# Attention scores in fewer shapes: decode queries laid out block-diagonally, prompt products alternating between halves

## The reference

```python
# differential attention: two score maps per head, each over 64 of the 128 head columns
a = probs(q[..., :64], k[..., :64]) - lam * probs(q[..., 64:], k[..., 64:])
out_da = a @ v
# multi-head latent attention: 128 columns without rotation and 64 rotated ones, the rotated key shared by all heads
k_m = concat([kv[..., :128], broadcast(k_rope)], axis=-1)
s = (q_m @ k_m.T) * 192 ** -0.5
out_mla = softmax(mask(s)) @ v_m
```

## Time and profile before

| what | value |
|---|---|
| median of three runs | 2510.61 us (2506.28 to 2514.45) |
| profiled execution, first to last instruction (its span) | 2504.7 us |
| TensorE busy | 2453.5 us, 98% of the span |
| chain of work that ended last, TensorE's share | 95% |
| VectorE, ScalarE, GpSimd busy | 1186.1, 801.0, 138.6 us |
| 16 DMA engines, share of the span on the weights' queue | 41.8% |
| mean granted TensorE clock | 0.992 |

### The profile page before, as it was taken

The page is one execution under the profiler, slowest core; times in us unless marked ns, Lnnn a source line. Parts: engine busy times, 40 slices in busy tenths (PEclk is TensorE's granted clock), DMA queues, the critical chain, the costliest instruction groups (busy, mean ns, idle before and its releaser), DMA issues.

```text
span 2504.7 us, 36768 instructions
## 1 busy us (share of the span) xinstructions
PE 2453.5 (98%) x16307; PEld 2389.8 (95%) x16307; DVE 1186.1 (47%) x892; ACT 801.0 (32%) x686; POOL 138.6 (6%) x59
## 2 busy tenths in 40 slices
PE   7999999999999999999999989999999999999998
PEld 5999999999999999989899669999999999999998
DVE  6444444444444447345484226444444444444445
ACT  3322322232323224333333224323322332233223
POOL 2000000000000001000000001000000000000001
PEclk9999999999999999999999899999999999999999
DMA  5444444444444444515153113444444444444441
GB/s 193 152 152 151 151 150 145 145 147 149 150 151 151 151 150 152 162 62 179 55 151 119 42 43 118 152 152 151 150 145 147 146 150 150 151 151 151 151 147 64
DMA packets 178896, 345.98 MB, mean 138 GB/s; under 512 B 10383, under 2 KB 17046, under 8 KB 178518
## 3 DMA queue, kind: packets, MB, share of 16 engines
q1 hardware_dynamic: 175942, 337.11, 41.8%
q0 software_dynamic: 2160, 7.60, 0.9%
q10 hardware_dynamic: 736, 0.41, 0.1%
HBM read 339.45 MB, written 5.65 MB: 138 GB/s over the span
## 4 chain that ended last, share of the span: by engine, by line
PE 95%; DVE 3%; ACT 1%; DMA 0%; issue 0%; SPq 0%; DVEq 0%; ACTq 0%
PE ps L1202 29%; PE ps L1203 29%; PE ps L1204 29%; DVE mov_lo L822 2%; DVE w_lo L805 1%; PE ps L1554 1%; PE ps L1553 1%; PE ps L1383 1%; PE ps L1381 0%; DMA work<-in_x_sample 0%; PE ps L1278 0%; PE ps L1564 0%; PE ps L1412 0%; PE ps L1579 0%; PE ps L1428 0%; PE ps L1238 0%
## 5 line engine op out<-in xcount | busy, mean ns | idle before, releaser
L1202 PE MATMUL ps<-mov_hi,w_hi 128*128 128x320 f32 x3568 | 1108.3, 311 | 9.6 <-DVE w_lo L805 8.6
L1203 PE MATMUL ps<-mov_lo,w_hi 128*128 128x320 f32 x3568 | 1104.4, 310 | 0.0
L1204 PE MATMUL ps<-mov_hi,w_lo 128*128 128x320 f32 x3568 | 1104.2, 309 | 0.0
L805 DVE TENSOR_TENSOR w_lo<-raw,w_hi 128x2048 fp32r<-128x2048 f32 x313 | 717.3, 2292 | 744.7 <-ACT w_hi L499 744.6
L499 ACT CAST w_hi<-raw 128x2048 fp32r<-128x2048 f32 x313 | 596.8, 1907 | 1429.0 <-PE ps L1204 1428.9
L1202 PEld LDWEIGHTS ps<-mov_hi,w_hi 128*128 128x128 f32 x3568 | 671.7, 188 | 12.7 <-issue 10.3
L1203 PEld LDWEIGHTS ps<-mov_lo,w_hi 128*128 128x128 f32 x3568 | 671.6, 188 | 0.5
L1204 PEld LDWEIGHTS ps<-mov_hi,w_lo 128*128 128x128 f32 x3568 | 671.5, 188 | 0.0
L1202 PE MATMUL ps<-h_hi,w_hi 128*128 128x320 f32 x1488 | 462.9, 311 | 4.7 <-DVE h_lo L894 4.7
L1203 PE MATMUL ps<-h_lo,w_hi 128*128 128x320 f32 x1488 | 462.4, 311 | 0.0
L1204 PE MATMUL ps<-h_hi,w_lo 128*128 128x320 f32 x1488 | 462.3, 311 | 0.0
(11 more groups left out here) (193 smaller groups left out, 835.9 us busy)
## 6 DMA issues: line engine op xcount, KB each, us to landing
raw<-in_ffn_w_gate SPq DMA_DIRECT2D x88, 1024.0 KB, 5.2
raw<-in_ffn_w_up SPq DMA_DIRECT2D x88, 1024.0 KB, 5.2
raw<-in_ffn_w_down SPq DMA_DIRECT2D x88, 1024.0 KB, 5.1
raw<-in_w_in SPq DMA_DIRECT2D x28, 1024.0 KB, 5.3
raw<-in_w_out SPq DMA_DIRECT2D x16, 1024.0 KB, 5.1
raw<-in_mla_w_uq SPq DMA_DIRECT2D x12, 256.0 KB, 4.2
raw<-in_w_in SPq DMA_DIRECT2D x4, 640.0 KB, 4.1
work<-in_x_prompt SPq DMA_DIRECT2D x2, 1024.0 KB, 6.4
```

The lines of the kernel that those rows point to most:

```text
L805: dve.tensor_tensor(w_lo[:, n % SPLIT_SLOTS, :], raw[:, n % RAW_SLOTS, :], w_hi[:, n % SPLIT_SLOTS, :].bitcast(F32), ALU.subtract).then_in ...
L1202: pe.matmul(out, w[0], x[0], start=first, stop=False)
L1203: pe.matmul(out, w[0], x[1], start=False, stop=False)
L1204: return pe.matmul(out, w[1], x[0], start=False, stop=last)
```

## The change

For differential attention the decode queries of a head are laid out once as a block-diagonal 128 x 128 matrix in a new region `D_QD` (half 0's 64 rows in columns 0 to 63, half 1's in columns 64 to 127, the rest zero). GpSimd zeroes the region once per half of the heads, after the cache transposes that used it are drained; ScalarE makes two copies into it; TensorE waits for them (`qd_set`) before the first head's scores. The products over the cache and over the new keys are then one of 128 rows each, where there were two of 64 rows, and they come first. The four prompt products follow, in turn half 0 and half 1. For the latent heads VectorE makes such a matrix of the rotated decode queries (`M_QRD`) with one memset and two copies, and `mla_scores` is put in another order: the four unrotated prompt products, the four unrotated decode products (which alternate between the two column halves), two products of 128 rows for the rotated decode part of both heads, and the four rotated prompt products, alternating between row halves.

```diff
--- before.py
+++ after.py
@@ -108,9 +108,10 @@
 F_GS, F_H, F_SQ, F_ACC, F_V, F_T = 6144, 7424, 8704, 9984, 11264, 11584
 D_QT, D_KT, D_VTOK, D_CKT, D_CV, D_P, D_AT, D_DG, D_CST, D_O0 = (
     0, 1280, 2560, 4096, 6144, 8192, 10880, 11584, 12160, 14208)
-D_VT, D_KTOK, D_O1 = D_CST, D_P, D_P
+D_VT, D_KTOK, D_O1, D_QD = D_CST, D_P, D_P, D_CST + 1280
 M_QN, M_QR, M_KN, M_VM, M_KR, M_P, M_AT, M_DG = 0, 2560, 3840, 7168, 10752, 11584, 12928, 14336
 M_CQ, M_CKV, M_KRAW, M_SQ, M_V, M_Y, M_T, M_CTOK = 0, 3840, 4480, 4800, 6080, 6400, 6720, 9472
+M_QRD = 14976
 M_SQ2, M_CCT, M_CCKV, M_CKR, M_RT = 7168, 8192, 11584, 12608, 13120
 PW = 1344
 
@@ -196,6 +197,8 @@
         job_ready = sem("job_ready")
         job_drained = sem("job_drained")
 
+        qd_zero = sem("qd_zero")
+        qd_set = sem("qd_set")
         scores_ready = sem("scores_ready")
         biased = sem("biased")
         max_ready = sem("max_ready")
@@ -461,6 +464,9 @@
 
                     pool.wait_ge(job_drained, 10 * hf + 3)
                     store_tokens([D_KTOK + UC * t for t in range(3)], UC, UC * hf, kp, ks, k_stored)
+
+                    pool.wait_ge(job_drained, 10 * hf + 7)
+                    pool.memset(wk(D_QD, UC), 0.0).then_inc(qd_zero, 1)
                     pool.wait_ge(job_drained, 10 * hf + 10)
                     store_tokens([D_VTOK + UC * t for t in range(3)], UC, UC * hf, vp, vs, v_stored)
 
@@ -649,6 +655,13 @@
                     for hh in range(HB):
                         n = 10 * hf + 3 + hh
                         drain_job(n, wk(D_CKT + PAST * hh, PAST), ps[:, job_bank(n), :])
+                    act.wait_ge(qd_zero, hf + 1)
+                    act.wait_ge(drained, GR_Z + 3 * hf + 1)
+                    for half in range(2):
+                        d = slice(HALF * half, HALF * half + HALF)
+                        last = act.copy(wk3(D_QD, 4, P, d)[:, :, DEC * half:DEC * half + DEC],
+                                        wk3(D_QT, 4, T, d)[:, :, SEQ:T])
+                    last.then_inc(qd_set, 1)
                 if j == 3:
                     da_exps(HB * hf)
 
@@ -1120,11 +1133,18 @@
                 dve.wait_ge(unit_used, U_UQ + j + 1)
                 dve.tensor_copy(wk3((M_QR, M_QN, M_QN + 4 * T)[j], 4, T), bank4(GR_UQ + j)).then_inc(drained, 1)
             next_lo(U_OA2)
+            dve.wait_ge(o_lo_done, 2)
+            link(dve.memset(wk(M_QRD, 4 * P), 0.0))
             dve.wait_ge(swap_ready, 2)
             dve.tensor_tensor(wk3(M_RT, 4, T), bank4(GR_ROPE), over(sin, 4), ALU.mult).then_inc(drained, 1)
             link(dve.tensor_tensor(wk3(M_QR, 4, T), wk3(M_QR, 4, T), over(cos, 4), ALU.mult))
             dve.wait_ge(drained, GR_ROPE + 1)
-            dve.tensor_tensor(wk(M_QR, 4 * T), wk(M_QR, 4 * T), wk(M_RT, 4 * T), ALU.add).then_inc(roped, 1)
+            link(dve.tensor_tensor(wk(M_QR, 4 * T), wk(M_QR, 4 * T), wk(M_RT, 4 * T), ALU.add))
+            for half in range(2):
+                d = slice(ROPE * half, ROPE * half + ROPE)
+                last = dve.tensor_copy(wk3(M_QRD, 4, P, d)[:, :, DEC * half:DEC * half + DEC],
+                                       wk3(M_QR, 4, T, d)[:, :, SEQ:T])
+            last.then_inc(roped, 1)
             dve.wait_ge(n_hi, 2)
             dve.tensor_tensor(latents(h_lo)[:, :, 0:T], wk3(M_CKV, 2, T), latents(h_hi)[:, :, 0:T].bitcast(F32),
                               ALU.subtract)
@@ -1375,13 +1395,15 @@
 
                         pe.wait_ge(biased, h)
                     hh, b = h % HB, scores_half(hf)
-                    for half in range(2):
-                        d = slice(HALF * half, HALF * half + HALF)
-                        q, k = wk(D_QT + T * hh, T, d), wk(D_KT + T * hh, T, d)
-                        pe.matmul(ps[:, b + half, 0:SEQ], q[:, P:SEQ], k[:, 0:SEQ], start=True, stop=True)
-                        pe.matmul(ps[:, b + half, SEQ:PH], q[:, 0:P], k[:, 0:P], start=True, stop=True)
-                        pe.matmul(ps[d, b + 2, :], q[:, SEQ:T], wk(D_CKT + PAST * hh, PAST, d), start=True, stop=True)
-                        ins = pe.matmul(ps[d, b + 3, 0:DEC], q[:, SEQ:T], k[:, SEQ:T], start=True, stop=True)
+                    qd = wk(D_QD + P * hh, P)
+                    pe.matmul(ps[:, b + 2, :], qd, wk(D_CKT + PAST * hh, PAST), start=True, stop=True)
+                    pe.matmul(ps[:, b + 3, 0:DEC], qd, wk(D_KT + T * hh + SEQ, DEC), start=True, stop=True)
+                    for at, rows, keys in ((0, slice(P, SEQ), SEQ), (SEQ, slice(0, P), P)):
+                        for half in range(2):
+                            d = slice(HALF * half, HALF * half + HALF)
+                            q, k = wk(D_QT + T * hh, T, d), wk(D_KT + T * hh, T, d)
+                            ins = pe.matmul(ps[:, b + half, at:at + keys], q[:, rows], k[:, 0:keys],
+                                            start=True, stop=True)
                     ins.then_inc(scores_ready, 1)
 
 
@@ -1395,6 +1417,7 @@
                     turn_cache(hh)
                 z_unit(3 * hf + 2, 2)
                 pe.wait_ge(job_drained, 10 * hf + 7)
+                pe.wait_ge(qd_set, hf + 1)
                 da_scores(HB * hf)
                 z_unit(3 * hf + 2, 3)
 
@@ -1541,17 +1564,32 @@
 
                         pe.wait_ge(exp_done, c)
                     pr = c - HEADS
+                    news, olds = slice(SEQ, T), slice(T, NTOK)
+                    blocks = ((0, slice(P, SEQ), slice(0, SEQ)), (SEQ, slice(0, P), slice(0, P)))
+
+                    def qn(half, q):
+                        return wk(M_QN + T * (2 * pr + half), T)[:, q]
+
+                    def kn(half, k):
+                        return wk(M_KN + NTOK * (2 * (pr % 2) + half), NTOK)[:, k]
+
                     for half in range(2):
-                        d = slice(64 * half, 64 * half + 64)
-                        qn = wk(M_QN + T * (2 * pr + half), T)
-                        kn = wk(M_KN + NTOK * (2 * (pr % 2) + half), NTOK)
-                        qr, kr = wk(M_QR + T * pr, T, d), wk(M_KR, NTOK, d)
-                        for out, q, k in ((ps[:, half, 0:SEQ], slice(P, SEQ), slice(0, SEQ)),
-                                          (ps[:, half, SEQ:PH], slice(0, P), slice(0, P)),
-                                          (ps[d, 2, :], slice(SEQ, T), slice(T, NTOK)),
-                                          (ps[d, 3, 0:DEC], slice(SEQ, T), slice(SEQ, T))):
-                            pe.matmul(out, qn[:, q], kn[:, k], start=True, stop=False)
-                            ins = pe.matmul(out, qr[:, q], kr[:, k], start=False, stop=True)
+                        for at, q, k in blocks:
+                            pe.matmul(ps[:, half, at:at + k.stop], qn(half, q), kn(half, k), start=(at == 0), stop=False,
+                                      skip_group_check=True)
+                    for bank, k in ((2, olds), (3, news)):
+                        for half in range(2):
+                            d = slice(64 * half, 64 * half + 64)
+                            pe.matmul(ps[d, bank, 0:k.stop - k.start], qn(half, news), kn(half, k), start=True,
+                                      stop=False, skip_group_check=True)
+                    for bank, k in ((2, olds), (3, news)):
+                        pe.matmul(ps[:, bank, 0:k.stop - k.start], wk(M_QRD + P * pr, P), wk(M_KR, NTOK)[:, k],
+                                  start=False, stop=True, skip_group_check=True)
+                    for at, q, k in blocks:
+                        for half in range(2):
+                            d = slice(64 * half, 64 * half + 64)
+                            ins = pe.matmul(ps[:, half, at:at + k.stop], wk(M_QR + T * pr, T, d)[:, q],
+                                            wk(M_KR, NTOK, d)[:, k], start=False, stop=True, skip_group_check=True)
                     ins.then_inc(scores_ready, 1)
 
                 def mla_transpose(c):
```

## The result

The changed kernel takes 2473.78 us (median of four runs, 2472.91 to 2483.58), beside 2509.59 us for the kernel before (median of four): a ratio of 0.9871 with a 95% interval of 0.9847 to 0.9895. The profiled execution has a span of 2472.3 us, 32.4 less than before's 2504.7. The remaining 3.4 us lie in where the two profiled executions fall among their runs: the median is 4.9 us above before's span and 1.5 above the span after.

A forecast was written before the change was run, and what follows sets the result against it. TensorE's own list was taken as the bound: 9.0 us saved in differential attention plus 11.5 in latent, other engines at 0, make 20.5 off the 2510.6 median, so 2490 us, range 2480.5 to 2499.5.

The forecast's parts named there:

- bounds of the one unknown cost: Alternating array halves in both score routines: gain 13 us if each step costs a change of shape, 25 us if halves overlap.
- I take the middle, covered loads and no overlap: Score routines: products on alternating halves run one after another with loads hidden; four prompt products take 1.30 us.
- rival 2: Score routines: products on different halves of the array overlap, 25 us gain in all, 2485.5 us; chance 0.33.
- Where the softmax chain would take time back: Differential attention, `da_values`: TensorE waits 0.35 us for one head and 0.3 for the next, 0.65 us per half.
- 6 instead of 2: Sign in `da_values`: waits of some size for ScalarE's copies rise to 6 from 2, some 1.3 us more.
- The costs put at nothing: Added memsets and copies on GpSimd, ScalarE and VectorE: price 0; without cover up to 2 us and 1.5 us.
- The same total, plus or minus 4 us: Half-clock time over the run: total cost taken as unchanged, within 4 us, though where the stretches fall was unknown.
- Rival 5: Attention part: the half-clock mechanism alone makes the kernel slower, needing 56 more us at 1.2 GHz; chance 0.03.
- the case that it described: Score routines: alternating halves neither costs nor overlaps, 2490 us, own range 2485 to 2495; chance 0.42.

## Why the prediction was wrong

The step that failed is the choice in **bounds of the one unknown cost**: "I take the middle, covered loads and no overlap". The nearest rows were products of one shape on the whole array, each on the same 128 rows and columns as the one ahead of it. They say nothing on products that use different halves. The term that this put in the sum was 1.30 us for the four prompt products of a head or pair and 1.95 us for the four 64-wide ones; they take 0.76 and 1.03 us (0.85 and 1.12 with the drain behind them). The other end of that bound, rival 2, had been worked out and given 0.33; the groups by shape (5.6 instead of 11.1 us at the same count and mean) and the starts show that it is what happens.

*Rival 2's size.* It was priced as 25 us less, with the second record of one product beside the first of the next. The records pair fully: both halves start 7 ns apart and go on together. The 64-wide group of a pair takes 1.12 us (1367.33 to 1368.45), 1.03 without the drain, where rival 2 had 1.4; the rotated prompt group takes 0.85, 0.76 without it, where rival 2 had 0.9. So a pair gives 4.5 us instead of 2.88 (forecast) or 3.8 (rival 2): latent part 18.0 instead of 11.5.

*The heads.* From the product before it to the product behind it a head is shorter by 2.04 us instead of the forecast 1.39, and behind `da_transpose` by 1.77 instead of 1.19. Eight heads give 15.2, the waits take back 4.4, which leaves 10.8 beside the 10.7 from the starts, and 9.0 forecast. Where the softmax chain would take time back was right, at `da_values` of the first two heads of each half, and so was how it starts (VectorE's bias step with no idle time left). The waits are longer (1.49 and 0.75 us instead of 0.35 and 0.3), because TensorE's list moved up further than thought and VectorE's chain could not follow. "6 instead of 2" waits miscounts: the earlier trace rows has four, and they became eight.

*The costs put at nothing* were nothing: `qd_set` never waited, ScalarE's copies took 0.41 us each (0.4 estimated) and ended 3.2 us ahead of the scores, GpSimd's memset 0.53 us, VectorE's memset and copies 1.07 us (at most 1.5). VectorE's idle time behind them fell to 2.14 us where 1.4 was forecast.

*The clock.* "The same total, plus or minus 4 us" was forecast; it gave 3.7 us. Some 3 of them went with the old `da_scores` in the ten profiles. What in the old order brings the stretches at 1094 and 1224 us wasn't tried and stays open. The stretch at 941 us lies ahead of everything that was changed and comes and goes between runs of one kernel. Rival 5's "about 25 us" at 1.2 GHz in the two latent blocks is more than the 17 and 4 us read from the earlier trace rows, 21 in all; the forecast doesn't hang on it.

*Adding up:* 20.5 forecast, 6.5 more from the pairs and 1.7 more from the heads make 28.7; the clock's 3.7 make the 32.4 us of the spans; 3.4 us are where the profiled executions lie among the runs: 35.8. The forecast for the case that it described was sound: the kernel that has everything except the overlap gained 17.7 us (2507.26 less 2489.55). Its added changes of shape were priced at 3.4 to 4.4 us, and 20.5 less these is 16.1 to 17.1. That its time is also nearly the forecast 2490 is luck in part, as these changes and a base 3 us faster offset each other.

The Trainium skill ("TensorE: Matmul & The Clock Gate", Part 3: Packing small matmuls — row/col tiling) says that products on different row or column groups run concurrently. The trace agrees for products of one shape, with 7 ns between the starts, and not for the neighbours of different shape in the kernel before (0.20 us). I had held against rival 2 that the old trace has no overlap of records; it had no neighbours of one shape on different halves, so it was no evidence against the rule. The same section also says that products start strictly in program order; the kernels without alternation differ, and the measurement decides: there half 1's first product starts 13 ns behind half 0's first, ahead of half 0's second.

## What to carry to other kernels

When products use only half of TensorE's rows or columns, put all those of one shape together, so that both halves are in the same run, and let the halves alternate when each has more than two products there: with five of each in a row, half by half, most ran alone (3.55 us, where all one after another would take 3.98); alternation itself was run with two of each only. Here grouping alone was worth 33 us of 2507, and packing two halves into one block-diagonal operand added nothing to it. Compare busy time with count and mean in the groups by shape: it shows at once whether products overlap. Where the nearest row of a trace can't show an effect by its construction, its silence is not evidence against it, and the forecast shouldn't lean on it.

## What the runs showed of the hardware that was not expected

- Two float32 products of one shape on the two row halves, the two column halves, or opposite quarters of the array ran fully side by side, 7 ns apart, each at the pace it has alone (the second record of a 64x256 product starts 320 ns behind its first in both kernels; the profile's means are 428 ns for 64x256 and 618 ns for 128x512 in both). The column halves and the quarters did so although both products write the same bank, on different partitions (line 1583: 8.6 to 4.3 us; the quarters: 17.1 to 8.6 us).
- They need not stand directly behind one another: past one waiting product of the other half the partner started 13 ns behind instead of 7. Past two none was seen to start; whether their number, their length or something else sets that reach is open.
- Two products of another shape between them end it (11.1 and 8.6 us busy again), and neighbours on different halves with different shapes didn't overlap in the kernel before (0.20 us between the starts). Whether one product of another shape between two of one shape ends it wasn't run by itself.
